# One FFN down-step per feature block with its weight splits in between, constant products around each norm's row sums, and the last two squares added by TensorE

## What is computed

```python
def rmsnorm(x, g):
    y = x32 * lax.rsqrt(jnp.mean(x32 * x32, axis=-1, keepdims=True) + RMS_EPS)
def modulate(z, g, shift, scale):
    return rmsnorm(z, g) * (1.0 + scale) + shift
def swiglu(h, wi, wo):
    a, u = jnp.split(h @ wi, 2, axis=-1)
    return (jax.nn.silu(a) * u) @ wo
x = x + 0.5 * m[2] * swiglu(modulate(x, norm_g[l, 0], m[0], m[1]), ffn1_wi[l], ffn1_wo[l])
```

## Time and profile before

| what | value |
|---|---|
| median of 3 runs | 3329.41 us (3328.49 to 3330.61) |
| profiled execution | 3326.68 us, its span 3324.9 us |
| TensorE busy | 3118.8 us, 94% of the span |
| VectorE busy | 1895.4 us, 57% |
| ScalarE busy | 1025.0 us, 31% |
| mean granted clock of TensorE | 0.965 of full speed |
| loaded from HBM | 360.51 MB, 109 GB/s |

### The profile page before, as it was taken

How to read it: one execution, slowest core, us unless ns; L and a number is a source line. 1 busy time by engine, 2 the same in 40 slices (tenths; PEclk the granted TensorE clock), 3 DMA queues, 4 the chain that set the end, 5 groups by cost and what they waited for, 6 DMA issues and landing times.

```text
span 3324.9 us, 36571 instructions
## 1 busy us (share of the span) xinstructions
PE 3118.8 (94%) x14791; PEld 2502.0 (75%) x14802; DVE 1895.4 (57%) x2720; ACT 1025.0 (31%) x1479; POOL 10.1 (0%) x23
## 2 busy tenths in 40 slices
PE   7999999897889999899988999889998998899998
PEld 6788888776667888778877788678887764577886
DVE  7876554645555544566656554566665555654344
ACT  3212222335442222322224222332223434432222
POOL 0000000000000000000000000000000000000000
PEclk8999999998999999999999999989999999899999
DMA  6433432110024443256522443235551210122321
GB/s 220 151 114 117 143 114 94 44 51 10 1 97 138 165 137 104 95 171 213 180 103 76 146 158 120 83 108 182 187 195 50 81 57 1 53 87 95 102 96 51
DMA packets 101843, 365.00 MB, mean 110 GB/s; under 512 B 11246, under 2 KB 12542, under 8 KB 101420
## 3 DMA queue, kind: packets, MB, share of 16 engines
q1 hardware_dynamic: 100636, 357.94, 31.8%
q0 software_dynamic: 1040, 4.71, 0.4%
HBM read 360.51 MB, written 2.10 MB: 109 GB/s over the span
## 4 chain that ended last, share of the span: by engine, by line
PE 86%; DVE 8%; ACT 3%; issue 1%; DMA 0%; SPq 0%; POOL 0%; DVEq 0%; ACTq 0%; POOLq 0%
PE ps L192 24%; PE ps L194 24%; PE ps L193 24%; PE ps L196 4%; PE ps L197 2%; DVE WL L184 1%; PE ps L526 1%; ACT WH L179 1%; DVE RAW L1291 1%; PE ps L2336 1%; PE ps L2576 1%; DVE SQ L594 0%; DVE XT L834 0%; PE ps L2676 0%; DVE DUMP L305 0%
## 5 line engine op out<-in xcount | busy, mean ns | idle before, releaser
L192 PE MATMUL ps<-HH,WH 128*128 128x512 f32 x2464 | 979.8, 398 | 28.3 <-DVE HL L583 21.4
L194 PE MATMUL ps<-HH,WL 128*128 128x512 f32 x2464 | 968.0, 393 | 0.0
L193 PE MATMUL ps<-HL,WH 128*128 128x512 f32 x2464 | 968.0, 393 | 0.0
L179 ACT ACTIVATE WH<-RAW 128x1024 fp32r<-128x1024 f32 x456 | 456.7, 1047 | 553.0 <-PE ps L194 410.7
L184 DVE TENSOR_TENSOR WL<-RAW,WH 128x1024 fp32r<-128x1024 f32 x456 | 538.4, 1220 | 86.2 <-ACT WH L179 86.0
L192 PEld LDWEIGHTS ps<-HH,WH 128*128 128x128 f32 x2464 | 468.1, 190 | 136.1 <-issue 33.5
L193 PEld LDWEIGHTS ps<-HL,WH 128*128 128x128 f32 x2464 | 468.3, 190 | 100.1 <-issue 4.6
L194 PEld LDWEIGHTS ps<-HH,WL 128*128 128x128 f32 x2464 | 467.7, 190 | 100.1
L834 DVE SCALAR_TENSOR_TENSOR XT<-ps,DER,XT 128x512 f32<-128x512 f32 x512 | 342.6, 682 | 271.1 <-PE ps L194 256.9
L192 PE MATMUL ps<-GH,WH 128*128 128x512 f32 x1056 | 413.9, 392 | 19.1 <-DVE XT L834 14.3
L775 DVE TENSOR_TENSOR S<-S,ps 128x512 f32<-128x512 f32 x132 | 90.7, 687 | 569.3 <-PE ps L194 569.3
(11 more groups left out here) (358 smaller groups left out, 2392.3 us busy)
## 6 DMA issues: line engine op xcount, KB each, us to landing
RAW<-in_w_modt SPq DMA_DIRECT2D x200, 512.0 KB, 4.3
RAW<-in_ffn_wi SPq DMA_DIRECT2D x176, 512.0 KB, 4.5
RAW<-in_ffn_wo SPq DMA_DIRECT2D x88, 512.0 KB, 4.7
RAW<-in_w_gu SPq DMA_DIRECT2D x88, 512.0 KB, 4.3
RAW<-in_w_in SPq DMA_DIRECT2D x44, 512.0 KB, 3.6
RAW<-in_w_down SPq DMA_DIRECT2D x44, 512.0 KB, 4.3
RAW<-in_w_out SPq DMA_DIRECT2D x16, 512.0 KB, 4.6
STG<-in_w_modt SPq DMA_DIRECT2D x10, 512.0 KB, 12.4
```

Source lines behind the costliest of these rows:

```text
L179: act.e.activation(u.hi, u.ld.view, ACT.Copy).then_inc(u.hi_done.sem, 1)
L192: pe.e.matmul(out, wh, x[0], start=first, stop=False)
L193: pe.e.matmul(out, wh, x[1], start=False, stop=False)
L194: m = pe.e.matmul(out, wl, x[0], start=False, stop=last)
```

## The change

Six edits, told one after the other.

1. **`Down` becomes eight steps.** `DownPart(down, d)` does block d on all engines. After d = 1, 3 and 5 the list gets one weight split of the next job, so DVE has them between its additions to x. A next `Up` has two weights, so two splits are placed. For all other jobs the splits stay before the job. `ModLoad` of the next row is now ahead of the two weight loads instead of behind them.
2. **The last two squares** (blocks 6 and 7) are no longer added by DVE. `RstdSum` sums three tiles (SA, and both SQ) into the same bank: 12 products of 6x128 in place of 4, 18 in place of 6 with the context.
3. **`Root`** (the table load of ACT) stands after the square of block 6 instead of 7.
4. **`Busy(n)`** issues n products of constants (128x128 by 128x256, float32) into bank 3, whose result nobody reads. Five stand after the row sums and five after the spread of every norm but the last; four in the pooling mixer before its last addition; in the first model's final norm two after each of the first seven blocks, each pair waiting for that block.
5. **At the start** `ModMul` 7 moves ahead of the spread, with 6 constant products behind it and 8 behind the spread.
6. **The first loads** are in another order: the pairs for rows 2 and 3 (`load_dot`, `load_mul`) come before the third and fourth parts of x.

```diff
-        if k:
+        if 0 < k < 6:
             self.add[k] = P.sqfree[k % 2] = P.s["sum_add"].next()
-            P.sat = self.add[k]
         if k == 7:
+            P.sat = [(P.SA, self.add[5]), (P.SQ[:, 0, :], self.sq[6]), (P.SQ[:, 1, :], self.sq[7])]
+        if k == 6:
             self.root = Root(P)
...
-        if k == 7:
+        if k == 6:
             self.root.scalar(act)
...
+class Busy(Step):
...
+    def tensor(self, pe):
+        P = self.P
+        pe.wait_ge(*self.after)
+        for _ in range(self.n):
+            pe.e.matmul(P.banks[3][:, 0:256], P.ID, P.K[:, 0:256], start=True, stop=True)
...
-        for q in range(self.nq):
-            m = pe.e.matmul(out, P.Z11[:, 5 - q:11 - q], P.SA[:, q * 128:(q + 1) * 128], start=q == 0, stop=True,
-                            skip_group_check=q > 0)
+        for i, (tile, ready) in enumerate(self.sat):
+            pe.wait_ge(*ready)
+            for q in range(self.nq):
+                m = pe.e.matmul(out, P.Z11[:, 5 - q:11 - q], tile[:, q * 128:(q + 1) * 128], start=i + q == 0, stop=True,
+                                skip_group_check=i + q > 0)
...
-            ahead = self.split(main[at][0]) if at < len(main) else (self.split(following) if following else None)
+            todo, ahead = list(main[at][0] if at < len(main) else following or []), []
+
+            def take():
+                if todo:
+                    ahead.extend(self.split([todo.pop(0)]))
+
+            if len(job) == 2:
+                while todo:
+                    take()
             if more:
                 self.add(ModLoad(*more))
-            job[1](units)
-            units = ahead
+            if len(job) == 2:
+                job[1](units)
+            else:
+                job[1](units, take)
+            units = ahead or None
...
             load_dot(2)
+            load_mul(2)
             load_x(2)
+            load_dot(3)
+            load_mul(3)
             load_x(3)
...
             mul(6)
+            muled = mul(7)
+            self.add(Busy(self, 6))
             self.add(RstdSpread(self, W // 128))
-            muled = mul(7)
+            self.add(Busy(self, 8))
...
+        self.add(Busy(self, 5))
         self.add(RstdSpread(self, nq))
+        self.add(Busy(self, 5))
...
-                def run(units):
-                    self.over = self.add(Down(F, fs, units, sums if fs[-1] == NF - 1 else None)).done[7, len(segs) - 1]
-                return ([wo[f] for f in fs], run)
+                def run(units, split_ahead):
+                    down = Down(F, fs, units, sums if fs[-1] == NF - 1 else None)
+                    self.over = down.done[7, len(segs) - 1]
+                    for d in range(8):
+                        self.add(DownPart(down, d))
+                        if d in (1, 3, 5):
+                            split_ahead()
+                return ([wo[f] for f in fs], run, "in pieces")
```

More of the change, by code:

```diff
@@ L818, in scalar @@
     def scalar(self, act):
-        if self.sums:
-            for d in range(8):
-                self.sums.square(act, d)
+        if self.down.sums:
+            self.down.sums.square(act, self.d)
     def vector(self, dve):
-        F, P = self.F, self.P
+        w, d = self.down, self.d
+        F, P = w.F, w.P
         dve.wait_ge(*P.modt[F.mi, 2])
-        for d in range(8):
-            for n, (c0, c1, j) in enumerate(F.segs):
-                out = P.banks[self.bank[d, n]]
-                x = P.XT[:, d, c0:c1]
-                dve.wait_ge(*self.done[d, n])
-                for i, o in enumerate([out] if n == 0 else [out[:, 0:TC], out[:, TC:2 * TC]]):
-                    if i:
-                        dve.wait_ge(*self.evac[d, n][0])
-                    dve.e.scalar_tensor_tensor(x, o, P.mod_g(F.mi, d, j), x, ALU.mult, ALU.add).then_inc(self.evac[d, n][i].sem, 1)
-            if self.sums:
-                self.sums.late(dve, d)
+        for n, (c0, c1, j) in enumerate(F.segs):
+            out = P.banks[w.bank[d, n]]
+            x = P.XT[:, d, c0:c1]
+            dve.wait_ge(*w.done[d, n])
+            for i, o in enumerate([out] if n == 0 else [out[:, 0:TC], out[:, TC:2 * TC]]):
+                if i:
+                    dve.wait_ge(*w.evac[d, n][0])
+                dve.e.scalar_tensor_tensor(x, o, P.mod_g(F.mi, d, j), x, ALU.mult, ALU.add).then_inc(w.evac[d, n][i].sem, 1)
@@ L839 @@
+        if w.sums:
+            w.sums.late(dve, d)
 class Proj:
@@ L2966, in start, with rstd_of @@
             return [muled, last]
-    def rstd_of(self, nq):
+    def rstd_of(self, nq, ahead=0, last=False):
+        if ahead:
+            self.add(Busy(self, ahead))
         self.add(RstdSum(self, nq))
+        if last:
+            self.add(RstdSpread(self, nq))
+            return
+        self.add(Busy(self, 5))
         self.add(RstdSpread(self, nq))
+        self.add(Busy(self, 5))
     def norm_tiles(self, ctx, two):
@@ L3022, in final_norm @@
     def final_norm(self, gname, again):
-        self.rstd_of(T // 128)
-        self.add(FinalNorm(self, gname, Sums(self, T) if again else None))
+        self.rstd_of(T // 128, last=not again)
+        final = self.add(FinalNorm(self, gname, Sums(self, T) if again else None))
+        if again:
+            for k in range(7):
+                self.add(Busy(self, 2, final.done[k]))
     def advance(self, lag):
@@ L3130, in mixer_pool @@
             mean(3)
+            self.add(Busy(self, 4))
             last = add(3)
```

47 lines of the change are left out of this document (27 added, 20 removed).

## The result

The changed kernel takes 3273.31 us, the median of 4 runs (3271.92 to 3276.42), against 3328.95 us of the kernel before beside it (3326.74 to 3330.61). The ratio is 0.9835, 95% interval 0.9818 to 0.9852. It is 55.6 us faster; 59.5 us and 3270.0 us were forecast, and the result lies in the range. The profiled execution took 3272.06 us, its span 3270.3 us, at a mean granted clock of 0.983 in place of 0.965.

What follows compares the result with a forecast made beforehand. TensorE was taken to bound the kernel nearly everywhere, with gains only where it idles or its clock is low. Parts of 24.3, 4.6, 29.3 and 1.3 us sum to 59.5, so 3329.4 becomes 3270 us; range 3258 to 3300.

Steps and rivals of the forecast that it cites:

- Part 1: Down in FFNs: additions ahead of weight splits remove TensorE's waits for XT and one clock fall; 24.3 us.
- the pace of 2.6 us in 2.7: Down without context: VectorE's two additions and one WL take 2.6 us in 2.7 us of products, so nothing stops.
- Part 2: Row sums before each norm: twelve products start at once, 2.80 us in place of 3.28; 4.6 us in all.
- Cost at most 0.1, under cover of the twelve sums: Row sums: moving the table load ahead of the last square delays that square by at most 0.1 us.
- Part 3: Norms: constant products keep full clock, speeding products behind the norm, spreads and the first model's final norm; 29.3 us.
- the reason given for it: Norms: sums of 6 columns seem to count as work for the clock, so full clock was expected through the norms.
- The largest term, 18 us: First 48 products behind eight norms: clock shortfall 1.53 in sum times 13 us, less VectorE's limits, saves 18 us.
- Part 4: Start: ModMul 7 moved into idle time gains 1.0 us, a shorter wait for loads 0.3; 1.3 us.
- A falling clock: Norms: clock falls anyway, constant products restore it before the norm's products; 3300 us, chance 0.10.
- Down's rival: Down: VectorE falls behind or next Up waits for WL, half of Part 1 lost; 3282 us, chance 0.08.
- The table load: Row sums: last square some 1.3 us late, 1.1 us lost at each of seven places; 3278 us, chance 0.04.
- The slower side: Norms: clock falls during row sums and stays down, 5.2 us lost at each of nine; 3351 us, chance 0.03.

Runs made afterwards that it cites:

- e1: Changed kernel with the next job's weight splits ahead of the whole Down again: 3303.73 us, ratio 0.9921.
- e5: Kernel before the change, with only Down in eight steps and the splits in between: 3299.74 us, ratio 0.9905.
- e7: e6 with chunk 21 last for blocks 0 and 1 in last Down of FFNs without context, four more constant products with context: 3269.98 us.
- e4: Changed kernel with the same number of constant products, using 6 columns of weights in place of 128: 3273.92 us, ratio 0.9826.
- a0: Changed kernel run again unaltered, on the same chip as e1 to e3: 3276.60 us, ratio 0.984.
- e6: Changed kernel with ScalarE's table load back behind the square of block 7: 3271.54 us, ratio 0.982.
- e3: Changed kernel with VectorE adding the last two squares again, so four row sums; constant products stay: 3284.06 us, ratio 0.9862.
- e2: Changed kernel with Busy issuing no constant products; the twelve row sums stay: 3292.53 us, ratio 0.9888.
- e11: e7 run once more without an edit, beside e10 on one chip: 3271.62 us, ratio 0.9824.
- e9: e7 plus ten constant products once in the second model's mixer, between the waits for the queries' and keys' splits: 3266.08 us, ratio 0.9808.
- e10: As e9, but the ten constant products stand ahead of both waits: 3262.54 us, ratio 0.9796.

## Why the prediction was right

**Part 1, Down in eight steps (24.3).** Right in mechanism, small by 3 to 5 us: 27.1 by e1, 29.5 by e5. The forecast took the waits alone, 2.9 us for an FFN, and 3.5 came back. Nothing of VectorE's was late next, as the pace of 2.6 us in 2.7 said. Here is VectorE in the first Down of stage 3, against the earlier trace rows:

```profile
1388.97 0.69 DVE L794 TENSOR_TENSOR GL<-S,GH 128x512 fp32r<-128x512 f32 x1 [0.76 <-ACT GH L774]
1389.58 1.42 DVE L856 SCALAR_TENSOR_TENSOR XT<-ps,DER,XT 128x512 f32<-128x512 f32 x2
1390.92 1.22 DVE L184 TENSOR_TENSOR WL<-RAW,WH 128x1024 fp32r<-128x1024 f32 x1
```

The additions start on GL's end, and the WL behind them. With context one wait of 0.59 us is left of an allowed 0.8. The GL waits stayed at 4.8 us, because the last group starts straight behind its Up; e7 confirms that reason by removing them.

**Part 2, the row sums (4.6).** The step that failed here is "Cost at most 0.1, under cover of the twelve sums". It took from the timeline of before that the square of block 6 ends 0.6 us before the last product. So it did there, since VectorE was idle between its additions. In the changed kernel one WL stands between them too, and at the end of stage 2 VectorE runs behind it without a gap up to block 6:

```profile
1326.87 1.23 DVE L184 TENSOR_TENSOR WL<-RAW,WH 128x1024 fp32r<-128x1024 f32 x1 [1.05 <-ACT WH L179]
...
1330.53 0.74 DVE L856 SCALAR_TENSOR_TENSOR XT<-ps,DER,XT 128x512 f32<-128x512 f32 x1
```

Block 6's addition ends at 1331.27, only 0.6 us before the last product, where that of before ended 1.25 ahead of it. The square is late by as much, the table load starts at 1331.96 and not 0.6 us earlier, and the square of block 7 at 1333.36, 1.48 us behind the last product and not 0.9. ScalarE at the end of stage 3, where a mixer follows, shows the other case:

```profile
1703.03 0.63 ACT L404 ACTIVATE SQ<-XT 128x512 f32<-128x512 f32 x1 [1.40 <-DVE XT L856]
1703.68 1.28 ACT L376 ACT_TABLE_LOAD   x1
```

The square ends 0.6 us before the last product (1704.25), as the forecast had it, and the sums take 2.79. e1, where the splits stand ahead of Down again, has sums of 2.79 us behind every FFN, and 3.36 behind the two mixers. So the sum for part 2 was right behind FFNs where part 1 doesn't reach into it, and each part was worked out on the timeline without the other. Behind the mixers, where no FFN's timeline holds, the table load holds up the square by itself. The gain is 3.28 less 3.14 behind three FFNs, less than nothing behind two mixers (3.36) and 0.5 at two places; with 0.8 once and 0.3 once where the sums had run at the low clock, part 2 came out near 2.4 us. No drain is seen behind the table load: Root starts 0.01 us behind its end (1333.25). The Trainium skill ("ScalarE: Activation LUTs", What ACT_TABLE_LOAD costs) would have the switch take some 1.4 us more; the trace doesn't agree, and the measurement decides.

**Part 3, constant products and clock (29.3).** The clock held in nine of ten norms, and e4 bears out the reason given for it. But the part came to some 21 to 23 us. These sizes were off.
- The largest term, 18 us for the products behind the norms, came to 13.8: from the first product to the end of the 48th it is 102.2 us in sum over eight norms before and 88.4 after. The forecast had the 48 products end 10.8 us after the first at full clock. TensorE in the norm between stages 2 and 3, behind the first product at 1341.38:

```profile
1342.82 0.47 PE L192 MATMUL ps<-HH,WH 128*128 128x512 f32 x1
...
1352.88 1.02 PE L261 MATMUL ps<-CC,K 128*128 128x512 f32 x2
```

  The first seven blocks of six products follow each other at 1.44 us, which is VectorE's pace of 1.45 and not 1.35. The last HL is there 9.4 us after the first product, as forecast, but the block ahead of the last one started only at 1350.07, so the last one starts at 1351.51 and not 0.7 us earlier. L261, the operation behind the 48, starts 11.5 us after the first product. It was 13.2 before (1362.24 to 1375.47): 1.7 us gained where 2.4 were counted. The shortfall of the clock times 13 us counts as lost some time that VectorE's pace takes at full clock too. This is read from the rows; no run varies VectorE's pace.
- The spread takes 1.15 us, not 1.04, 0.1 at nine places, and the one with context gains nothing (2.60 and 2.57 us): 8.3 us in place of 9.8.
- In stage 1's norm the clock fell for 6.8 us. The timeline of the changed kernel there, ScalarE and TensorE:

```profile
607.64 0.52 ACT L1055 ACTIVATE CB<-CF 128x384 bf16<-128x384 f32 x1 [3.88 <-DMA CF<-in_cb]
608.07 0.29 ACT L473 ACTIVATE R<-R 6x128 f32<-6x128 f32 x1
```

```profile
605.79 2.43 PE L498 MATMUL ps<-K 128*128 128x256 f32 x10
610.33 2.57 PE L543 MATMUL ps<-R,SEL 6*128 6x128 f32 x12 [2.11 <-DVE R L485]
612.83 4.63 PE L498 MATMUL ps<-K 128*128 128x256 f32 x10
616.91 0.91 PE L192 MATMUL ps<-HH,WH 128*128 128x512 f32 x1
```

  The square root waits for ScalarE's copy of a table behind a transfer (3.88 us), the five constant products are over too early, and 2.11 us stay idle. The second five run at the low clock, and the first product waits for their end, 15.1 us behind the last one in place of 13.4 before. The forecast knew of this copy in part 2 and forgot it in part 3. What that cost stage 1 as a whole isn't shown. It gained 1.6 us here and lost 0.4 in a0; in e6 and e7 the clock didn't fall there, the first product came after 12.4 and 12.5 us, and the stage still took 360.0 and 360.1 us, against 359.1 before.
- In the first model's final norm 1.5 us were forecast between spread and second sum's end and 0.7 came. TensorE there, in the changed kernel:

```profile
2119.01 8.52 PE L498 MATMUL ps<-K 128*128 128x256 f32 x38
2127.46 1.04 PE L519 MATMUL ps<-SA,K 128*6 128x128 f32 x8
```

  Nineteen constant products stand without a gap, and the sums start on their end, 0.52 us after SA was there (2126.94). The forecast compared the pairs (0.87) with VectorE's pace of 1.4 us per block, and left out that the five behind the spread stand ahead of them.
- The second model's mixer gave some back: stage 7 gained 2.9 us, but its norm and first 48 products 3.5, so what follows lost 0.6. Its clock was low for 23.9 us from 2808.9 us on. That this is the cause isn't shown, since a0, with short falls, took 0.6 us longer still. It is inside the 4 us allowed for the mixers.

**Part 4, the start (1.3).** The 1.0 for ModMul 7 came, the 0.3 for the loads became a loss of about 0.6: some 0.4 us remain, too little to tell from scatter.

**The sum.** 27 to 29.5 for part 1 and 25 to 29 for the rest, against 24.3 and 35.2. Two errors of opposite sign, 3 to 5 us on one side and 6 to 10 on the other, meet in a forecast 3.3 us from the median: the mechanisms held, but that the total is so close is partly luck.

**The rivals.** A falling clock is refuted by the windows above. Down's rival is refuted by the waits for XT; the one longer wait for WL is in a mixer and comes in some executions only. The table load does hold up the last square, but for its own length and not for twice that. The slower side's mechanism exists: in e3 at four norms, about 1.3 us each, and in the changed kernel at one, that of stage 1, where the clock fell behind the sums. Nowhere does it last through a whole norm that has constant products.

## What to carry to other kernels

Where several engines work down one hand-written list, look at what stands between the last input of a waiting engine and the operation it waits for: two weight splits for a later job in front of an addition cost 27 us here, and moving them cost some tenths at the norms. Where the granted clock falls behind short waits, fill the wait itself with products whose result nobody reads, ahead of the wait's instruction and not behind it, and count their time against the shortest of the waits they must fit in. Work out the price of one edit on the timeline that the others leave behind: a wait of 0.69 us in front of each addition was gone once a split stood between them. Move a table load to the place where its engine has room for its whole length; "one operation earlier" can be in front of the one the others wait for.

## What the runs showed of the hardware

- Constant products with six columns of weights did as well as those with 128: in e4 the granted clock is 1.00 in the same windows, at 3273.92 us.
- Idle time alone doesn't tell whether the clock falls. 2.62 us of idle time ahead of the spread in e2 left it at full clock behind stages 2 and 5, and the same 2.63 us behind stage 6 did not (2.07 us); 2.11 us in stage 1's norm, behind the constant products, were followed by a fall at 610.8.
- The same stretch of work (2804 to 2835 us) ran at a clock of 0.56 in two executions of one program (e7, e11) and at 0.78 and 0.83 in two programs that differ from it by ten products 130 us earlier (e9, e10). The changed kernel had 0.61 there once and 0.83 in a0, without an edit between them.
- A constant product of 128x256 unsplit float32 takes 0.45 us in a row of nineteen (8.52 us) at full clock, and five with 6 columns take nearly what five with 128 do (2.32 and 2.42): its price is its length and not its width.
